# Score products of a first model's attention as two rounded products over stacked key parts

## The chip, the cores and the metric

One core of one Trainium2 chip runs the whole program. The metric is the device time of one execution in microseconds, the median of three executions: 3229.28 us before the change (3226.82, 3229.28 and 3235.23 us). PE is the matmul engine (TensorE), PEld its weight loads, DVE VectorE, ACT ScalarE, POOL GpSimd, SP SyncE. Lines such as L1209 are lines of the kernel before.

## The reference

Two models run one after the other. The first has two layers over 512 main tokens and 256 context tokens. Each layer normalises the tokens, projects them, and mixes them by two convolutions and two attentions; then follow an output projection and a feed-forward part of 16 experts. The change touches the attentions of the first model alone. Each has 4 query heads of 64 channels that share 2 key/value heads. One is global; the other sees keys at most 128 positions away, the context keys, and a learned sink logit:

```python
def gqa_attend(q, k, v, sink=None):
    s = jnp.einsum('bqkgd,bjkd->bkgqj', q, k).astype(jnp.float32) * (HEAD_DIM ** -0.5)
    ...
    p = jax.nn.softmax(s, axis=-1)
    ...
    return jnp.einsum('bkgqj,bjkd->bqkgd', p.astype(v.dtype), v)
def window_attention(q, k, v, kc, vc, sink):
    ...
    valid = (kpos >= 0) & (kpos < s) & (jnp.abs(qpos - kpos) <= WINDOW)
    s_loc = jnp.where(valid[None, :, None, None], s_loc, -jnp.inf)
    sl = jnp.broadcast_to(sink.reshape(N_KV_HEADS, GQ)[None, :, :, None, None].astype(jnp.float32),
                          s_loc.shape[:-1] + (1,))
    p = jax.nn.softmax(jnp.concatenate([s_loc, s_ctx, sl], axis=-1), axis=-1)
```

In the first layer the 256 context tokens are queries too; in the second they are keys alone.

## The kernel before

The program is a list of stages. The five engines walk through it each in its own order, fixed when the program is built, and meet only at semaphores. The change is in the stage `attend`, which occurs twice: layer 0 (281 to 451 us of the profiled execution) and layer 1 (1271 to 1398 us).

`attention_plan` cuts an attend stage into groups. A group is one kind (1 is the global attention, 0 the windowed one with masks and sink), one key/value head `g` with its two query heads, and either the 512 main queries (a main group) or the 256 context queries (a context group). Layer 0 runs eight groups, g0 to g7: the even ones main, the odd ones context, g0 to g3 of kind 1 and g4 to g7 of kind 0. Layer 1 runs four main groups, g0 and g1 of kind 1, g2 and g3 of kind 0. A group's work is:

- Row maxima, `row_scores` on PE and `maximum` on DVE (L2637, L2639). The scores are computed with queries as rows, one unit per query tile and head, and DVE takes the largest of each row. For main groups the operands are rounded copies in fp32r, k_round and q_round (L1171 global, L1175 windowed tiles with the mask product L1177, L1178 context keys); for context groups they are plain f32 (L1163). The units of a group are issued inside the steps of an earlier group: two groups earlier in layer 0, one in layer 1.
- The shift, `turn_shift` on PE (L1189) and `take_shift` on ACT: the negated maxima are turned into a row and copied (L1934) into row 64 of the queries, so that with the row of ones in the keys each score product subtracts the maximum by itself. For kind 0, two exponentials for the sink come first (L1932). PE waits for the copy before the group's first score product.
- Steps, one per tile of 128 keys, two context tiles first and then, in main groups, four main ones. `scores` on PE computes keys by queries in f32 for each head (L1209; L1202 in context groups), in windowed steps plus one mask product per edge, identity by band (L1213); `exponentials` on ACT (L1975) turns them to probabilities; `mix` on PE (L1230) multiplies the values by them, in f32. Scores of step n+1 are issued before the mix of step n. There are four score banks, two per step.
- The outcome: ACT copies the sums (L1953, L1954), DVE divides (L2678, L2680).

Between these, ACT and DVE compute a 31-tap convolution in their spare time: ACT makes products (L1964) that POOL adds up (L3311), DVE does the other half (L2663, L2666), one tap after each maximum and a few after each outcome. `round_operands` on ACT makes the rounded copies of main groups (L1940 keys, L1941 queries): before the first steps for g0 and the next main group, then in step 1 of a main group for a later one.

## Time and profile before

| what | value |
|---|---|
| timed executions | 3226.82, 3229.28, 3235.23 us |
| profiled execution, span from the first to the last instruction | 3215.5 us |
| attend, layer 0 | 281 to 451 us, 170 us |
| attend, layer 1 | 1271 to 1398 us, 127 us |
| PE busy in the whole span | 2983.4 us, 93% |
| DVE, ACT, POOL busy in the whole span | 1100.8, 737.7, 381.7 us |

The profile gives the profiled execution a span and no device time beside it; the median of the timed runs is 13.8 us longer than this span. The two attend stages are 297 us, 9% of the span. An f32 matmul stands in the trace as two records and an fp32r matmul as one; the trace writes f32 in the shape of both. The ends of matmuls are modelled, so a duration of one record is longer than the distance to the next.

### The profile page before, as it was taken

Reading aid. Unit: us, or ns where it says so; the run is one execution under the profiler, and the core shown is the slowest. Engines: PE = TensorE matmul, PEld = TensorE weight load, DVE = VectorE, ACT = ScalarE, POOL = GpSimd, SP = SyncE. Lnnn points to the kernel's source line nnn. Section 1 sums busy time; section 2 is a strip of 40 time slices with the busy share of each in tenths; the row PEclk is TensorE's granted clock in tenths of the full one; section 3 lists DMA queues with packets and bytes.
Section 4 is the critical chain, followed back from the end, with each engine's and each line's share of the span. In section 5 each row is a group of like instructions: output and inputs, shape, how many; then the busy total and the mean of one; then the engine's idle time right before and its main releaser. Section 6 shows DMA issues by size and latency. Waiting matters only on the chain.

```text
span 3215.5 us, 50344 instructions
## 1 busy us (share of the span) xinstructions
PE 2983.4 (93%) x21802; PEld 1880.8 (58%) x21802; DVE 1100.8 (34%) x1930; ACT 737.7 (23%) x1393; POOL 381.7 (12%) x494
## 2 busy tenths in 40 slices
PE   6999989699999998986988888999999999999999
PEld 3645556455555464554433333888865568678887
DVE  4124754211111244643222224322434463232242
ACT  3113651000000133541000002222322362222232
POOL 2022520122222121411000000000000000000000
PEclk8998989799999999997999999999999989999999
DMA  8930033899999810037999996122311202231130
GB/s 342 394 129 1 1 144 120 344 401 409 408 409 408 308 55 1 1 138 290 417 423 423 424 423 252 59 105 79 113 67 55 69 18 79 79 111 65 66 140 30
DMA packets 138400, 626.97 MB, mean 195 GB/s; under 512 B 12592, under 2 KB 19776, under 8 KB 82896
## 3 DMA queue, kind: packets, MB, share of 16 engines
q1 hardware_dynamic: 122064, 577.67, 44.8%
q0 software_dynamic: 16128, 46.18, 4.3%
q8 instruction: 172, 2.82, 0.4%
q14 instruction: 36, 0.29, 0.0%
HBM read 607.36 MB, written 16.45 MB: 194 GB/s over the span
## 4 chain that ended last, share of the span: by engine, by line
PE 42%; DMA 10%; DVE 2%; ACT 1%; issue 1%; SPq 0%; POOL 0%; DVEq 0%; ACTq 0%; POOLq 0%
PE bank L959 19%; DMA slots<-in_w_up_dram 10%; PE bank L1526 7%; PE bank L1714 4%; PE bank L1403 3%; PE bank L1630 3%; PE bank L1283 1%; PE bank L1647 1%; PE bank L1424 1%; PE bank L1658 0%; PE bank L1453 0%; PE bank L1648 0%; SPq L910 0%; PE bank L1060 0%; PE bank L1061 0%
## 5 line engine op out<-in xcount | busy, mean ns | idle before, releaser
L1403 PE MATMUL bank<-slots,HT 128*32 128x256 f32 x8192 | 478.0, 383 | 52.4 <-DMA slots<-in_w_gate_dram 24.2
L1403 PEld LDWEIGHTS bank<-slots,HT 128*32 128x32 f32 x8192 | 265.6, 111 | 269.0 <-issue 62.6
L959 PE MATMUL bank<-hT_high,chunk_high 128*128 128x512 f32 (+2 forms) x736 | 285.1, 387 | 5.3 <-DVE hT_low L2500 5.3
L959 PE MATMUL bank<-hT_high,low_slots 128*128 128x512 f32 (+2 forms) x736 | 287.1, 390 | 0.0
L959 PE MATMUL bank<-hT_low,chunk_high 128*128 128x512 f32 (+2 forms) x736 | 285.5, 388 | 0.0
L2091 ACT ACTIVATE arena<-bank 128x512 f32<-128x512 f32 x32 | 19.1, 597 | 756.2 <-PE bank L1403 433.8
L959 PE MATMUL bank<-slots,HT 128*128 128x512 f32 (+4 forms) x544 | 180.3, 491 | 7.2 <-issue 5.8
L2843 DVE TENSOR_TENSOR arena<-bank,arena 128x512 f32<-128x512 f32 x32 | 22.1, 692 | 441.9 <-ACT arena L2091 441.9
L959 PEld LDWEIGHTS bank<-hT_high,chunk_high 128*128 128x128 f32 x736 | 139.0, 189 | 35.7 <-DVE hT_low L2500 5.7
L959 PEld LDWEIGHTS bank<-hT_low,chunk_high 128*128 128x128 f32 x736 | 138.8, 189 | 32.4 <-issue 0.2
L959 PEld LDWEIGHTS bank<-hT_high,low_slots 128*128 128x128 f32 x736 | 138.7, 188 | 29.7
L2979 DVE TENSOR_TENSOR arena<-bank,arena 128x512 f32<-128x512 f32 x44 | 30.4, 691 | 355.0 <-PE bank L959 355.0
L1424 PE MATMUL bank<-arena,HT 128*32 128x512 f32 x1280 | 148.1, 599 | 3.1 <-DVE HT L2838 3.1
L959 PEld LDWEIGHTS bank<-slots,HT 128*128 128x128 f32 x544 | 96.3, 193 | 84.3 <-issue 69.2
L1526 PE MATMUL bank<-down_high,ffnT_low 128*128 128x512 f32 x352 | 137.6, 391 | 0.0
L1526 PE MATMUL bank<-down_high,ffnT_high 128*128 128x512 f32 x320 | 125.8, 393 | 0.0
L1526 PE MATMUL bank<-low_slots,ffnT_high 128*128 128x512 f32 x320 | 124.2, 388 | 0.0
L1412 PE MATMUL bank<-slots,HT 128*32 128x256 f32 x2048 | 122.4, 379 | 0.0
L2884 DVE TENSOR_TENSOR X<-X,bank 128x1024 f32<-128x1024 f32 x60 | 70.0, 1207 | 149.1 <-PE bank L1453 149.1
L3311 POOL TENSOR_TENSOR HT<-HT,arena 128x512 f32<-128x512 f32 (+1 forms) x90 | 108.1, 1201 | 76.2 <-ACT arena L1964 66.5
L2164 ACT ACTIVATE arena<-bank 128x512 f32<-128x512 f32 x44 | 26.4, 600 | 363.8 <-PE bank L959 363.7
L2961 DVE TENSOR_TENSOR low_slots<-slots,chunk_high 128x1024 fp32r<-128x1024 f32 x88 | 103.4, 1217 | 2.6 <-ACT chunk_high L2142 2.6
(453 smaller groups left out, 4897.4 us busy)
## 6 DMA issues: line engine op xcount, KB each, us to landing
slots<-in_w_gate_dram SPq DMA_DIRECT2D x128, 1024.0 KB, 19.5
slots<-in_w_up_dram SPq DMA_DIRECT2D x128, 1024.0 KB, 21.7
arena<-in_w_down_dram SPq DMA_DIRECT2D x80, 1024.0 KB, 23.3
arena<-in_ada_w_dram SPq DMA_DIRECT2D x48, 1024.0 KB, 9.1
X<-in_w_down_dram SPq DMA_DIRECT2D x32, 1024.0 KB, 18.3
slots<-in_w_in_dram SPq DMA_DIRECT2D x15, 2048.0 KB, 8.9
slots<-in_ffn_w_gate_dram SPq DMA_DIRECT2D x10, 2048.0 KB, 8.5
slots<-in_ffn_w_up_dram SPq DMA_DIRECT2D x10, 2048.0 KB, 8.9
```

The source lines that it names most:

```text
L959: mm = pe.matmul(out_, lhsT, rhs, start=(n == 0), stop=(n == len(pairs) - 1))
L1283: mm = pe.matmul(bank[:, b + j, :], y, part, start=(k == OUT_WHOLE[0]), stop=(k == OUT_LATE[-1]))
L1403: mm = pe.matmul(bank[32 * j:32 * j + 32, 2 + n, 256 * g:256 * g + 256], xT[:, 64 * k + 32 * g:64 * k + 32 * g + 32], columns(w[:, c, :], ...
L1412: mm = pe.matmul(bank[32 * j:32 * j + 32, 4, 256 * n:256 * n + 256], xT_c[:, 32 * k:32 * k + 32], columns(w[:, c, :], j), start=(k == 0 an ...
L1424: mm = pe.matmul(bank[32 * j:32 * j + 32, 5, :], actT[half][:, 2 * q + c, lo:lo + 32], w[:, c, 512 * h:512 * h + 512], start=(q == 0 and c ...
L1526: mm = pe.matmul(bank[:, b, :], x, w_parts[part][:, 512 * half:512 * half + 512], start=(k == 0 and m == 0), stop=(k == F_CHUNKS - 1 and m ...
L1630: mm = pe.matmul(bank[:, j, :], HT[:, k, tile_cols(i)], w[:, k, :], start=(k == 0), stop=(k == KD - 1))
L1647: pe.matmul(bank[:, b, 0:qt * P + P], qT[rows, h, tile_cols(qt)], kT[rows, h, 0:qt * P + P], start=True, stop=False)
L1714: mm = pe.matmul(bank[:, b + n, :], w, x, start=(k == ks[0] and part == 0), stop=(k == ks[-1] and part == 2))
L2884: dve.tensor_tensor(X[:, t, :], X[:, t, :], flat_bank[:, at_spread:at_spread + D], ALU.add).then_inc(sem["spread_taken"], 1)
L2961: dve.tensor_tensor(ffn_columns(low_flat(unit), c), ffn_columns(slot_of(unit), c), chunk_high[:, g % SPLIT_RING, :, :].bitcast(F32), ALU.s ...
L3311: pool.tensor_tensor(dst, other, products[:, n % 4, 0:hi - lo], ALU.add).then_inc(sem["tap_added"], 1)
```

## The change

Each score product, f32 keys by f32 queries, becomes two fp32r products into the same bank. Keys and queries are each split into a rounded part (high) and the rest (low). `k_parts` holds the low part of the keys in partitions 0 to 63 and their high part in 64 to 127; `q_round`, and for context queries the new `c_round`, hold the high part of the queries twice, in both halves. The first product takes all 128 partitions and gives (low + high keys) by high queries. The second takes the high keys with their row of ones by the low queries `q_low`, whose row 64 is now the shift, 65 partitions. Low by low is left out. `k_parts` and `q_low` lie over the f32 keys and queries.

For this, ACT makes two more copies per main group and two for each context group, and DVE subtracts (`low_parts`): two subtractions for a main group, one for a context group. The maxima of context groups use rounded operands too, all maxima leave out row 64, and the mask products use fp32r copies of identity and band, which ACT makes once. `take_shift` copies first, and the sink exponentials read that copy. PE no longer waits for the sink exponentials before the next group's maxima. POOL no longer clears the queries' row 64. The scratch for POOL's DMA descriptors goes from its default to 8192 bytes a partition.

```diff
+        c_round = rounded("c_round", slots_at, first_slots("qkv")[0] % SLOTS * SLOT + 4 * NTOK, 2, 2, CTX)
+        k_parts = rounded("k_parts", arena_at, at_moe, 2, 2, NTOK)
+        q_low = [rounded(f"q_low{l}", slots_at, unit % SLOTS * SLOT, 2, HEADS, NTOK) for l, unit in enumerate(first_slots("w_out"))]
+
+        def q_high(st, group, rows, j):
+
+            if group.main:
+                return q_round[st.layer][rows, group.kind, group.heads + j, :]
+            return c_round[rows, group.turn, j, :]
...
-                    if unit is group.units[0] and group.main:
-                        mains = sum(other.main for other in groups[:group.number + 1])
-                        pe.wait_ge(sem["rounded"], st.at("rounded", 2 * mains))
+                    if unit is group.units[0]:
+                        pe.wait_ge(sem["rounded"], st.at("rounded", group.split_by))
                     if unit is group.units[0] and group.number >= ahead:
                         pe.wait_ge(sem["shift_done"], st.at("shift_done", group.number))
-                        before = 2 * sum(other.kind == 0 for other in groups[:group.number])
-                        if before:
-                            pe.wait_ge(sem["sink_row"], st.at("sink_row", before))
-                    kT = K_ext[0:HD + 1, group.kind, group.g, :]
+                    kT = k_round[st.layer][0:HD, group.kind, group.g, :]
                     if not group.main:
                         for j in range(2):
-                            mm = pe.matmul(bank[:, b, CTX * j:CTX * j + CTX], q_ext[0:HD + 1, group.kind, group.heads + j, tile_cols(qt)],
+                            mm = pe.matmul(bank[:, b, CTX * j:CTX * j + CTX], q_high(st, group, slice(0, HD), j)[:, tile_cols(qt - ST)],
                                            kT[:, SEQ:NTOK], start=True, stop=True)
                         mm.then_inc(sem["rowmax_full"], 1)
...
                     if one.first:
+                        pe.wait_ge(sem["w_split"], st.at("w_split", group.split_by))
                         pe.wait_ge(sem["shift_done"], st.at("shift_done", group.number + 1))
-                    keys = K_ext[0:HD + 1, group.kind, group.g, tile_cols(one.kt)]
+                    both_parts = k_parts[:, group.kind, group.g, tile_cols(one.kt)]
+                    high_part = k_round[st.layer][0:HD + 1, group.kind, group.g, tile_cols(one.kt)]
...
                         if j is None:
-                            pe.matmul(bank[:, b, :].rearrange("p (a n) -> p a n", a=2), keys,
-                                      q_ext[0:HD + 1, group.kind, group.heads:group.heads + 2, SEQ:NTOK],
-                                      start=True, stop=True).then_inc(sem["score_full"], 1)
+                            out_ = bank[:, b, :].rearrange("p (a n) -> p a n", a=2)
+                            pe.matmul(out_, both_parts, c_round[:, group.turn, :, :], start=True, stop=False)
+                            pe.matmul(out_, high_part, low[0:HD + 1, group.kind, group.heads:group.heads + 2, SEQ:NTOK],
+                                      start=False, stop=True).then_inc(sem["score_full"], 1)
                             continue
                         edges = []
                         if group.kind == 0 and one.kt < ST:
                             edges = [(t, 0 if t < one.kt else 1) for t in (one.kt - 1, one.kt + 1) if 0 <= t < ST]
-                        mm = pe.matmul(bank[:, b, 0:one.hi - one.lo], keys, q_ext[0:HD + 1, group.kind, group.heads + j, one.lo:one.hi],
-                                       start=True, stop=not edges)
+                        out_ = bank[:, b, 0:one.hi - one.lo]
+                        pe.matmul(out_, both_parts, q_high(st, group, slice(0, P), j)[:, one.lo:one.hi], start=True, stop=False)
+                        mm = pe.matmul(out_, high_part, low[0:HD + 1, group.kind, group.heads + j, one.lo:one.hi], start=False, stop=not edges)
                         for t, side in edges:
                             lo = P * t - one.lo
-                            mm = pe.matmul(bank[:, b, lo:lo + P], ident[:, :], band[:, side, :], start=False, stop=t == edges[-1][0])
+                            mm = pe.matmul(bank[:, b, lo:lo + P], ident_high[:, :], band_high[:, side, :], start=False, stop=t == edges[-1][0])
                         mm.then_inc(sem["score_full"], 1)
...
                 def take_shift(group):
 
                     n = group.queries[1] - group.queries[0]
+                    shift = q_low[st.layer][HD:HD + 1, group.kind, group.heads:group.heads + 2, group.queries[0]:group.queries[1]]
                     act.wait_ge(sem["shift_full"], st.at("shift_full", group.number + 1))
+                    act.activation(shift, bank[0:1, 4:6, 0:n], ACT.Copy).then_inc(sem["shift_done"], 1)
                     if group.kind == 0:
...
+                        act.wait_ge(sem["shift_done"], st.at("shift_done", group.number + 1))
                         for j in range(2):
-                            act.activation(rows[HD:HD + 1, j, 0:n], bank[0:1, 4 + j, 0:n], ACT.Exp, scale=HD ** -0.5,
-                                           bias=sink[0:1, st.layer, group.heads + j:group.heads + j + 1]).then_inc(sem["sink_row"], 1)
-                    act.activation(q_ext[HD:HD + 1, group.kind, group.heads:group.heads + 2, group.queries[0]:group.queries[1]],
-                                   bank[0:1, 4:6, 0:n], ACT.Copy).then_inc(sem["shift_done"], 1)
+                            act.activation(rows[HD:HD + 1, j, 0:n], shift[:, j, :].bitcast(F32), ACT.Exp, scale=HD ** -0.5,
+                                           bias=sink[HD:HD + 1, st.layer, group.heads + j:group.heads + j + 1]).then_inc(sem["sink_row"], 1)
 
                 def round_operands(group):
 
                     kind, g = group.kind, group.g
-                    act.activation(k_round[st.layer][0:HD + 1, kind, g, :], K_ext[0:HD + 1, kind, g, :], ACT.Copy)                       .then_inc(sem["rounded"], 1)
-                    act.activation(q_round[st.layer][0:HD + 1, kind, 2 * g:2 * g + 2, :], q_ext[0:HD + 1, kind, 2 * g:2 * g + 2, 0:SEQ],
-                                   ACT.Copy).then_inc(sem["rounded"], 1)
+                    q = q_ext[0:HD, kind, 2 * g:2 * g + 2, group.queries[0]:group.queries[1]]
+                    if group.main:
+                        act.activation(k_round[st.layer][0:HD + 1, kind, g, :], K_ext[0:HD + 1, kind, g, :], ACT.Copy)\
+                           .then_inc(sem["rounded"], 1)
+                        q_to = q_round[st.layer][:, kind, 2 * g:2 * g + 2, :]
+                    else:
+                        q_to = c_round[:, group.turn, :, :]
+                    act.activation(q_to[0:HD, :, :], q, ACT.Copy).then_inc(sem["rounded"], 1)
+                    if group.main:
+                        act.wait_ge(sem["rounded"], st.at("rounded", group.split_by - 1))
+                        act.activation(k_parts[HD:P, kind, g, :], K_ext[0:HD, kind, g, :], ACT.Copy).then_inc(sem["w_high"], 1)
+                    act.activation(q_to[HD:P, :, :], q, ACT.Copy).then_inc(sem["w_high"], 1)
...
-                to_round = [group for group in groups if group.main]
-                round_operands(to_round.pop(0))
+                round_operands(groups[0])
+                if ahead == 2:
+                    round_operands(groups[1])
                 take_shift(groups[0])
-                round_operands(to_round.pop(0))
+                round_operands(groups[ahead])
                 if ahead == 2:
                     take_shift(groups[1])
...
-                        if n == 1 and to_round and group.main:
-                            round_operands(to_round.pop(0))
+                        if n == 1 and group.number + ahead + 1 < len(groups):
+                            round_operands(groups[group.number + ahead + 1])
...
+                def low_parts(group):
+
+                    kind, g = group.kind, group.g
+                    cols = slice(*group.queries)
+                    heads = slice(group.heads, group.heads + 2)
+                    if group.main:
+                        dve.wait_ge(sem["w_high"], st.at("w_high", group.split_by - 1))
+                        dve.tensor_tensor(k_parts[0:HD, kind, g, :], K_ext[0:HD, kind, g, :], k_round[l][0:HD, kind, g, :].bitcast(F32),
+                                          ALU.subtract).then_inc(sem["w_split"], 1)
+                        high = q_round[l][0:HD, kind, heads, :]
+                    else:
+                        high = c_round[0:HD, group.turn, :, :]
+                    dve.wait_ge(sem["w_high"], st.at("w_high", group.split_by))
+                    dve.tensor_tensor(q_low[l][0:HD, kind, heads, cols], Q_ext(l)[0:HD, kind, heads, cols], high.bitcast(F32),
+                                      ALU.subtract).then_inc(sem["w_split"], 1)
+
...
                     for unit in group.units:
                         maximum(unit)
+                    if group.number == 0:
+                        low_parts(group)
...
-                    for unit in units:
+                    for n, unit in enumerate(units):
                         maximum(unit)
+                        if n == 1:
+                            low_parts(groups[group.number + 1])
...
-                step(pool.memset(Q_ext(st.layer)[HD:HD + 1, :, :, :], 0.0))
...
-    nc = bacc.Bacc("TRN2", target_bir_lowering=False, num_devices=1)
+    nc = bacc.Bacc("TRN2", target_bir_lowering=False, num_devices=1, dynamic_dma_scratch_size=8192)
```

On ACT in layer 0, around the steps of context group g1 (L1964 or L1991 are taps, L1975 or L2002 exponentials, L1934 or L1944 the shift of g3, L1953 and L1954 or L1980 and L1981 the outcome of g1), before:

```order
L1975 ACTIVATE arena<-bank 128x512
L1934 ACTIVATE slots<-bank 1x2x256
L1964 ACTIVATE arena<-arena,conv_b_w 128x512
L1975 ACTIVATE arena<-bank 128x512 x2
L1953 ACTIVATE arena<-bank 64x256
L1954 ACTIVATE HT<-bank 64x256
L1953 ACTIVATE arena<-bank 64x256
L1954 ACTIVATE HT<-bank 64x256
L1964 ACTIVATE arena<-arena,conv_b_w 128x512 x2
L1975 ACTIVATE arena<-bank 128x512 x2
L1940 ACTIVATE k_round_54<-arena 65x768
L1941 ACTIVATE q_round_56<-slots 65x1024
```

The same place after the change:

```order
L2002 ACTIVATE arena<-bank 128x512
L1944 ACTIVATE q_low_60<-bank 1x2x256
L1960 ACTIVATE k_round_54<-arena 65x768
L1965 ACTIVATE q_round_56<-slots 64x1024
L1968 ACTIVATE k_parts<-arena 64x768
L1969 ACTIVATE q_round_56<-slots 64x1024
L1991 ACTIVATE arena<-arena,conv_b_w 128x512
L2002 ACTIVATE arena<-bank 128x512 x2
```

The copies of main group g4 have moved from step 1 of g2 to step 1 of g1, ahead of the exponentials of g2's first step, and are four instead of two; in step 1 of g2 the two copies of context group g5 take their place.

On DVE in layer 0, at the maxima of context group g3 within g1 (TENSOR_REDUCE is a maximum, SCALAR_TENSOR_TENSOR 128x2 the negation, on HT a tap), after the change; before, the same rows stand there without L2717 and L2723:

```order
L2667 TENSOR_REDUCE small<-bank 128x2
L2694 SCALAR_TENSOR_TENSOR HT<-arena,conv_b_w,HT 128x256
L2667 TENSOR_REDUCE small<-bank 128x2
L2679 SCALAR_TENSOR_TENSOR small<-small 128x2 x2
L2717 TENSOR_TENSOR k_parts<-arena,k_round_54 64x768
L2723 TENSOR_TENSOR q_low_60<-slots,q_round_56 64x2x512
L2694 SCALAR_TENSOR_TENSOR HT<-arena,conv_b_w,HT 128x512
L2706 RECIPROCAL arena<-arena 128x512
```

The low parts of g2 stand behind the second maximum and its negation, ahead of the tap and of the division of g0's outcome.

On PE in layer 0, a windowed step of g4 with one unit of maxima around it, before:

```order
L1209 MATMUL bank<-slots,arena 128x384
L1213 MATMUL bank<-band,ident 128x128 x2
L1209 MATMUL bank<-slots,arena 128x384
L1213 MATMUL bank<-band,ident 128x128 x2
L1175 MATMUL bank<-k_round_54,q_round_56 128x128
```

and after:

```order
L1223 MATMUL bank<-q_round_56,k_parts 128x384
L1224 MATMUL bank<-q_low_60,k_round_54 128x384
L1227 MATMUL bank<-band_high,ident_high 128x128 x2
L1223 MATMUL bank<-q_round_56,k_parts 128x384
L1224 MATMUL bank<-q_low_60,k_round_54 128x384
L1227 MATMUL bank<-band_high,ident_high 128x128 x2
L1185 MATMUL bank<-k_round_54,q_round_56 128x128
```

Nothing has moved past anything else; each f32 score product is two rows.

## Rows read from the trace of the kernel before

**Rows 1.** The page: span, and busy time of each engine.

```profile
span 3215.5 us, 50344 instructions
PE 2983.4 (93%) x21802; PEld 1880.8 (58%) x21802; DVE 1100.8 (34%) x1930; ACT 737.7 (23%) x1393; POOL 381.7 (12%) x494
```

**Rows 2.** Stretches of layer 0's attend: length, PE, PEld, DVE, ACT, POOL busy, PEclk, DMA.

```profile
301.80:323.35 21.55, 21.55 (x59) 10.86 (x58) 13.07 (x20) 7.37 (x12) 0.33 (x1) 0.85 0.00 0
323.35:347.30 23.95, 22.00 (x80) 12.26 (x79) 17.05 (x24) 21.08 (x36) 15.13 (x12) 1.00 0.00 1
347.30:359.30 12.00, 12.00 (x55) 7.16 (x54) 9.52 (x13) 4.33 (x8) 7.89 (x6) 1.00 0.00 0
359.30:381.60 22.30, 17.65 (x59) 9.87 (x59) 19.21 (x24) 19.19 (x34) 14.54 (x10) 0.97 0.00 1
381.60:405.25 23.65, 23.60 (x113) 17.02 (x113) 13.97 (x22) 6.70 (x16) 9.65 (x10) 0.89 0.00 1
405.25:425.60 20.35, 16.73 (x43) 9.75 (x42) 13.34 (x17) 14.87 (x31) 6.44 (x8) 0.75 0.00 0
425.60:440.00 14.40, 14.40 (x62) 9.74 (x61) 0.49 (x1) 8.30 (x20) 8.89 (x13) 1.00 0.01 2
```

**Rows 3.** The same for layer 1's attend.

```profile
1286.70:1310.36 23.66, 23.66 (x62) 11.55 (x61) 13.84 (x19) 7.64 (x13) 0.00 (x0) 0.83 0.00 0
1310.36:1326.30 15.94, 15.94 (x57) 8.54 (x56) 10.37 (x13) 15.37 (x26) 10.90 (x9) 1.00 0.00 1
1326.30:1337.84 11.54, 11.54 (x53) 6.94 (x52) 8.85 (x12) 3.60 (x6) 5.84 (x4) 1.00 0.00 1
1337.84:1352.00 14.16, 12.60 (x46) 6.49 (x45) 13.83 (x11) 13.70 (x24) 9.82 (x7) 1.00 0.00 0
1352.00:1366.84 14.84, 14.79 (x89) 11.43 (x88) 9.21 (x12) 4.11 (x8) 8.31 (x6) 1.00 0.01 1
1379.00:1391.30 12.30, 12.30 (x55) 8.50 (x53) 0.66 (x1) 3.16 (x8) 1.68 (x3) 1.00 0.01 1
```

**Rows 4.** Groups of PE instructions: line, names, shapes, count, busy us, mean ns, idle before.

```profile
L1209 PE MATMUL bank<-slots,arena 65*128 65x512 f32 (+2 forms) x192 | 92.0, 592 | 3.7 <-ACT slots L1934 3.7
...
L1177 PE MATMUL bank<-band,ident 128*128 128x128 f32 x96 | 21.5, 307 | 0.0
...
L1213 PE MATMUL bank<-band,ident 128*128 128x128 f32 x96 | 16.4, 280 | 0.0
...
L1163 PE MATMUL bank<-arena,slots 65*128 65x256 f32 x32 | 11.3, 516 | 3.1 <-DVE small L2637 1.6 <-ACT slots L1934 1.5
```

**Rows 5.** PE in order of time: start, us, line, tile, shape, count.

```profile
395.19 0.61 PE L1213 MATMUL bank<-band,ident 128*128 128x128 f32 x4
...
462.29 0.39 PE L1283 MATMUL bank<-low_slots,out_y_high_a 128*128 128x512 f32 x1
462.52 0.39 PE L1283 MATMUL bank<-out_w_high,out_y_low 128*128 128x512 f32 x1
```

**Rows 6.** PE weight loads of an f32 product, in order of time.

```profile
468.02 0.19 PEld L1283 LDWEIGHTS bank<-slots,HT 128*128 128x128 f32 x1 [0.24 <-issue]
468.45 0.19 PEld L1283 LDWEIGHTS bank<-slots,HT 128*128 128x128 f32 x1 [0.24 <-issue]
```

**Rows 7.** ACT in order of time: the two rounded copies of a main group.

```profile
341.61 0.84 ACT L1940 ACTIVATE k_round<-arena 65x768 fp32r<-65x768 f32 x1
342.35 1.05 ACT L1941 ACTIVATE q_round<-slots 65x1024 fp32r<-65x1024 f32 x1
```

**Rows 8.** Groups of DVE instructions with two tensors from SBUF; the second in layer 0's attend.

```profile
L2592 DVE TENSOR_TENSOR arena<-arena,rope_cos 128x768 f32<-128x768 f32 x8 | 7.7, 958 | 0.3
...
L2680 DVE TENSOR_TENSOR HT<-HT,arena 128x512 f32<-128x512 f32 x4 | 4.0, 996 | 0.1
```

**Rows 9.** One microsecond at a time, PE alone: length, PE busy, PEclk.

```profile
378.00:379.00 1.00, 0.00 (x0) 1.00 0.00 0
...
380.00:381.00 1.00, 1.00 (x6) 0.57 0.00 0
```

20 lines of the change are left out of this document (15 added, 5 removed).

## The prediction

> **What bounds the kernel now.** I read the page first, then the two attend stages in stretches cut where the limiting engine changes, then the PE groups in them, then the distances between instructions. The span is 3215.5 us, and PE is busy in 93% of it [rows 1]. The stretches say more. In four of layer 0's seven, and in the stretches of layer 1 from 1286.70, 1310.36, 1326.30, 1352.00 and 1379.00, PE has hardly an idle moment [rows 2, 3]. But three other stretches have another limit. From 323.35 ACT is busy 21.08 of 23.95 us. From 359.30 ACT and DVE are busy 19.19 and 19.21 of 22.30 us, and PE only 17.65. From 1337.84 DVE and ACT are busy 13.83 and 13.70 of 14.16 us. From 1310.36 ACT has 15.37 of 15.94 us, so there PE and ACT are level. The change takes work from PE and gives work to ACT and DVE: it pays in the first sort of stretch and costs in the second.
>
> **What PE saves.** An f32 product is two records; loads of one in dense work stand 468.45 - 468.02 = 0.43 us apart for 512 columns [rows 6], so a product costs 0.86 us at full clock. An fp32r product of 512 columns is one record, and two of them start 462.52 - 462.29 = 0.23 us apart [rows 5]. Two of these in place of one f32 product save 0.40 us. By columns, 384 save 0.30 and 256 save 0.20. A maximum product of 256 columns goes from 0.43 to 0.12: 0.31. For a mask product, four f32 records take 0.61 us, and 0.28 of it is the length of the last [rows 4, 5]: 0.11 a record, 0.22 a product, and one fp32r record of 0.11 to 0.14 saves about 0.09.
> Counts: L1209 has 192 records, 96 products; by the plan these are 64 of 512 columns, 16 of 384 and 16 of 256. Context groups have 8 more of 512, L1163 has 16 products and the masks 96 (192 records) [rows 4]. So 72 x 0.40 + 16 x 0.30 + 16 x 0.20 + 16 x 0.31 + 96 x 0.09 = 50 us. About ten score products and half of L1163's run at half clock, where each saves as much again: 57 us in all. This is the most that can be had.
>
> **What ACT and DVE get.** A main group's copies cost 0.84 and 1.05 us, started 0.74 us apart [rows 7], so four take about 3.75 instead of 1.9. Two copies of a context group, half as wide as the queries' copy, take about 1.2. With eight main and four context groups that is 8 x 1.9 + 4 x 1.2 = 20 us more on ACT. On DVE a subtraction of 768 columns takes 0.96 us [rows 8] and one of 1024 columns, in proportion, 1.28: 2.2 us for each of eight main groups, about 0.65 for each of four context groups, 20 us in all. No row shows a subtraction of this shape on 64 partitions. A lower bound is the 2.2 us; for the upper one the L2680 row is nearest: with POOL at work its mean was 0.996 us for 512 columns, which makes 3.5 us. I take 2.2 and keep 3.5 for the range.
> The GPSIMD Engine Reference of the Trainium skill (section Specifications) says that POOL shares its SBUF interfaces with VectorE and contends with instructions that read two tensors from SBUF. The trace agrees with the L2680 row; were every subtraction to meet POOL, this would be the upper bound, some 5 us more in the sum.
>
> **Layer 0, by stretches** [rows 2].
> (a) To 323.35: PE bound. Context maxima at the front run at half clock: 8 products, 4 of them ahead of the first shift, save 2.5 us. Of g0's score products 12 stand here, six at half clock: 6 x 0.4 + 6 x 0.8 = 7.2. Against it, ACT has two more copies ahead of the first exponentials, 1.9 us. -8.
> (b) From 323.35: ACT bound. g4's copies come in whole (3.75), and g5's 1.2 stand where 1.9 stood; the wait for g3's shift behind PE shrinks by two products, 0.8. +2.3.
> (c) From 347.30: PE bound. Six score products (2.4) and some sixteen masks (1.4). -4.
> (d) From 359.30: ACT and DVE bound. g6's four copies (3.75) and g7's two (1.2) come in, 4.95 us; ACT was idle for 22.30 - 19.19 = 3.1 us of the stretch, and I let two of them take it up: +2.9. DVE's 2.2 us for g4 run beside that.
> (e) From 381.60: PE bound with DVE busy 13.97 of 23.65 and ACT 6.70, so the cover holds. Four products of 384, four of 256, two of 512, some 22 masks, part of it at half clock: -5.
> (f) From 405.25: a chain from ACT's outcome of g4 over one mix to the next shift; half a score pair at half clock: -1.
> (g) From 425.60: PE bound. Four of 384, four of 256, one of 512, fourteen masks: -3.5.
> Sum -16.3. The tail behind, ACT and DVE's last outcome, does not change.
>
> **Layer 1** [rows 3].
> (a) To 1310.36: by PE alone -5, but DVE binds before that. Its 13.84 us of maxima and taps begin only with the first mix, which stands several us into the stretch, and become 16.0 with the subtractions; the shift of g1 waits for the last maximum. What is left is the earlier start, as the first mix no longer stands behind f32 scores at half clock: -2.2.
> (b, c) 1310.36 to 1337.84: ACT gets 1.9 us more in (b), PE needs 1.2 us less in each beat of (c), DVE has 27.48 - 19.22 = 8.3 us idle, mostly at the front, and takes 2.2. -3.
> (d) From 1337.84: ACT and DVE bound, nothing added to either. 0.
> (e) From 1352.00: DVE 9.21 of 14.84, so 5.6 us idle, less 2.2: -3.4, PE's own saving here being 4.2.
> (f) 1366.84 to 1379.00: ACT bound: 0. (g) From 1379.00: -2.5 by products of 384 and 256 and the masks.
> Sum -11.1. Both layers: -27.4.
>
> **The clock.** PE idled all of 378 to 379 us, and from 380 the granted clock was at half, 1.2 of 2.4 GHz [rows 9]; the stretch from 381.60 has a mean of 0.89 [rows 2], so 2 x 0.11 x 23.65 = 5.2 us at half and 2.6 us lost. With PE faster and ACT not, PE will idle more in (b) and (d) of layer 0 and from 1310.36. I allow one more such fall, +2.4. Total -25: a span of 3190.5, and with the 13.8 us between the span and the median of 3229.28 us a time of 3204 us.
> The page TensorE: Matmul & The Clock Gate (section HAM oscillation) of the Trainium skill states the rule against this change: idle gaps throw the PE clock back to half, and work in bursts then runs cold again and again. Rows 9 agree on one gap; how many the change makes, no row shows.
>
> **No cost.** The copies of identity and band are two short ones on ACT in the projection stage, where it waits for PE. Dropping POOL's clearing frees an engine that was waiting. The smaller descriptor scratch has no row; POOL's DMAs are gathers and loads well apart, and I put nothing on it. If it held POOL up, the gathers of the experts would be late and the time after 451 us would grow.
>
> **Rivals.**
> (R1) The whole of PE's saving comes through, ACT and DVE hiding all: -57, 3172 us. For it: PE is hardly idle in four of seven stretches of layer 0 and in most of layer 1. Against: the full ACT and DVE in (b) and (d).
> (R2) ACT and DVE in series eat nearly all: their 20 us each fall on the path in turn wherever a group's shift waits for both, and PE's saving in PE-bound stretches is cut to what DVE leaves. Of layer 0's -22 in (a), (c), (e), (g) half stays, -11, with +5 and +5 in (b) and (d), and layer 1 comes to -5: -6 with subtractions at 3.5, 3223 us. For it: DVE's taps follow each maximum, whatever PE does.
> (R3) The clock, slower than before: PE, waiting for ACT in each group's front, stays at half clock into the PE-bound stretches. About 215 us of PE work are left in the two stages; each microsecond of it at half clock costs one more. From 27 us beyond what is cold now the gain is gone; if 50 us are, the time is 3229 - 27 + 50 = 3252 us. For it: rows 9. Against: the stretch from 323.35 has idle PE and a clock of 1.00.
> (R4) A product over rounded parts costs as much as an f32 record, 0.43: the scores then save nothing, and only masks and context maxima do, 14 us, against 7 us more of ACT where it binds, and 3 us of masks that it hides: 3225 us. The 0.23 of rows 5 speaks against it.
>
> **Chances and range.** Forecast 0.60, R1 0.08, R2 0.19, R3 0.08, R4 0.05. The forecast's own range is 3192 to 3217 (PE-bound stretches two thirds as good or a third better, subtractions at either bound, none or three more falls of the clock). The range of 8 in 10 reaches toward R1 and past R2: 3181 to 3226. 0.3% is 9.7 us, about what a measurement of this kernel tells from no change: faster than 3219.6 is nearly all of the forecast, R1, and a third of R2: 0.73. Within 0.3%: most of R2, a little of the forecast and of R4: 0.16. Slower: R3 and the rest: 0.11.
>
> **What would show it.** Distances of 0.23 us between the two products of a pair (against R4); L1209's 92 us of records replaced by some 192 records of fp32r; ACT busy nearly throughout the stretches that follow the shifts of g2 and g4 and these longer by 2 to 3 us; PE with gaps there, and half clock in one place more than before; DVE without idle time between maxima in g0 of layer 1; attend about 154 us in layer 0 and 117 in layer 1, plus the clock; everything outside the two stages as long as before. The prediction is wrong if the stages shrink by less than 10 or more than 40 us together, or if time changes after 451 us outside attend.

## The result and the profile after

The changed kernel took 3263.95 us, median of 4 runs (3247.02 to 3272.16); the kernel before took 3229.44 us beside it. The ratio is 1.0098, with a 95% interval of 1.0073 to 1.0123: slower by 1.0%, where the prediction said 3204 us. The profiled execution took 3272.16 us, 1.9 us more than its span. The page of the changed kernel, whose counterpart is [rows 1]:

```profile
span 3270.3 us, 50164 instructions
PE 3013.4 (92%) x21690; PEld 1892.7 (58%) x21690; DVE 1125.8 (34%) x1950; ACT 757.0 (23%) x1419; POOL 378.5 (12%) x492
```

PE has 112 records fewer and is busy 30 us longer than in [rows 1]. Of these, 13 us lie in the attends and 15 between them, and those 15 belong to the execution that [rows 1] shows, as the next lines tell. The changed kernel by stages (from the start of layer 0's attend to the end of layer 1's); columns as in [rows 2], and the row in the middle is what lies between the two attends:

```profile
277.60:460.30 182.70, 149.29 (x456) 86.98 (x456) 113.39 (x144) 106.86 (x193) 93.72 (x87) 0.79 0.01 3
460.30:1300.00 839.70, 784.68 (x8716) 438.76 (x8716) 221.40 (x453) 115.25 (x241) 139.07 (x204) 0.96 0.73 287
1300.00:1441.80 141.80, 127.24 (x368) 71.79 (x368) 82.38 (x86) 74.70 (x123) 59.54 (x44) 0.76 0.01 1
```

The same three stretches of a second profile of the kernel before (run e5_before_again), and the middle one of the first profile:

```profile
276.20:445.60 169.40, 150.33 (x520) 89.64 (x520) 100.46 (x133) 95.19 (x178) 88.71 (x87) 0.87 0.01 3
445.60:1284.20 838.60, 783.59 (x8716) 443.64 (x8716) 221.46 (x453) 115.19 (x240) 144.08 (x205) 0.96 0.74 288
1284.20:1407.70 123.50, 113.19 (x416) 65.86 (x416) 70.23 (x78) 67.78 (x115) 57.80 (x44) 0.90 0.01 1
```

```profile
448.50:1270.10 821.60, 769.74 (x8716) 431.43 (x8716) 221.44 (x453) 115.26 (x241) 144.08 (x205) 0.96 0.74 294
```

The attends grew by 13.3 and 18.3 us, together 31.6; the medians differ by 34.5. The middle is level, 839.7 against 838.6. The profile that the prediction read was a rare execution, some 18 us short in the middle, so its span lay 13.8 us under the median, and this belonged to that execution, not to what lies around a span.

Where the attends grew, by stretches that end at the same transposes (L1199, L1189 before): the one from 316.20 answers to [rows 2] from 323.35 to 359.30 (35.95 us), the one from 1341.90 to [rows 3] from 1310.36 to 1337.84 (27.48 us).

```profile
316.20:364.60 48.40, 40.58 (x117) 21.68 (x117) 28.31 (x39) 28.36 (x47) 23.43 (x17) 0.82 0.00 0
...
1341.90:1378.80 36.90, 36.28 (x97) 18.59 (x97) 21.92 (x26) 20.76 (x33) 16.38 (x12) 0.77 0.00 0
```

In the second one PE is idle for 0.62 us only, and yet it takes 9.4 us more. A granted clock of 0.77 means that 17 of its 36.9 us ran at half clock and lost 8.5. What is left, 27.8 us, is what the stretch took before at full clock (27.48). So PE's own work did not shrink as predicted, and a large part ran at half clock.

**One account for all runs.** The runs of the next section appear here already. I cut both attends at each change of the granted clock and read PE's busy time in every piece. The length is then a sum of three: PE's work at full clock (busy at full, plus half of busy at half), what the half clock cost (the other half), and PE's idle time. Work here is busy time, stalls inside it included. Both attends together, us, from one profile each; times are medians. "maxima" is the row count of the maximum products, "split" tells which engines did the split's work (unused: done, but PE does not read it; left out: not done), "cold" is what the half clock cost.

```
run                   maxima  split       time    length  work   cold  idle
before, 2nd profile   65      -           3230    292.9   233.5  30.1  29.4
changed               64      ACT, DVE    3264    324.5   211.7  64.9  47.9
e6  max64             64      -           3261    325.8   265.7  33.5  26.6
e8  masks, ctx        65      -           3224.5  286.6   218.2  38.6  29.9
e9  masks, ctx, 64    64      -           3274    343.4   245.1  69.8  28.6
e3  f32 scores        64      unused      3307    367.9   244.9  78.7  44.3
e4  no split          64      left out    3250    306.8   211.4  57.0  38.4
e7  65, no split      65      left out    3201    262.0   187.1  32.4  42.4
e12 ACT copies        65      ACT only    3209    270.6   187.4  34.3  49.0
e14 unwaited          65      unused      3234    285.8   187.5  41.9  56.5
e1  65 rows           65      ACT, DVE    3233    295.1   188.6  43.4  63.1
e10 65, f32 masks     65      ACT, DVE    3233    300.8   198.8  41.1  61.0
e11 keys later        65      ACT, DVE    3226    286.2   190.1  34.6  61.4
e13 POOL              65      ACT, POOL   3208    277.2   188.1  31.5  57.6
```

From before to the changed kernel: work -22 instead of the -50 of the prediction, half clock +35 instead of +2.4, idle +18.5. The sum is +31.6. One profile is one execution: outside the attends, where these kernels hardly differ, the sixteen profiled executions took between 2923 and 2947 us. Medians of times and lengths of single profiles can therefore differ by some 10 us.

### The profile page after: what moved, and what is told of

Its sections match the earlier page's. It is cut to its first block, busy times and chain, and to the rows that moved or that the text cites. A ratio compares the mean times of both kernels' runs of the same rounds, so it can differ in the third digit from the quotient of the medians.

```text
span 3270.3 us, 50164 instructions
## 1 busy us (share of the span) xinstructions
PE 3013.4 (92%) x21690; PEld 1892.7 (58%) x21690; DVE 1125.8 (34%) x1950; ACT 757.0 (23%) x1419; POOL 378.5 (12%) x492
## 4 chain that ended last, share of the span: by engine, by line
PE 42%; DMA 10%; DVE 2%; ACT 1%; issue 1%; SPq 0%; POOL 0%; DVEq 0%; ACTq 0%; POOLq 0%
PE bank L974 19%; DMA slots<-in_w_up_dram 9%; PE bank L1540 7%; PE bank L1728 4%; PE bank L1417 3%; PE bank L1644 2%; PE bank L1297 1%; PE bank L1661 1%; PE bank L1438 1%; DMA slots<-in_w_gate_dram 1%; PE bank L1672 1%; PE bank L1662 0%; PE bank L1467 0%; PE bank L1075 0%; PE bank L1076 0%
## 5 line engine op out<-in xcount | busy, mean ns | idle before, releaser
L1417 PE MATMUL bank<-slots,HT 128*32 128x256 f32 x8192 | 492.4, 385 | 54.9 <-DMA slots<-in_w_gate_dram 28.9
L1244 PE MATMUL bank<-arena 128*128 128x512 f32 (+2 forms) x224 | 121.5, 672 | 23.4 <-ACT HT L1981 15.6
L1426 PE MATMUL bank<-slots,HT 128*32 128x256 f32 x2048 | 130.0, 379 | 0.7
```

The costliest lines, as they stand in the source:

```text
L1244: mm = pe.matmul(bank[:, 6 + j, lo:hi], V_ext[:, one.kt, group.kind, at_v:at_v + P], p, start=one.first, stop=ends)
L1417: mm = pe.matmul(bank[32 * j:32 * j + 32, 2 + n, 256 * g:256 * g + 256], xT[:, 64 * k + 32 * g:64 * k + 32 * g + 32], columns(w[:, c, :], ...
L1426: mm = pe.matmul(bank[32 * j:32 * j + 32, 4, 256 * n:256 * n + 256], xT_c[:, 32 * k:32 * k + 32], columns(w[:, c, :], j), start=(k == 0 an ...
```

## Experiments

**Rows of the maxima.** The diff has one edit that the prediction gave no term: the maximum products multiply 64 rows (`0:HD`) where they multiplied 65. PE in one beat of the changed kernel at full clock, where windowed maxima are made: four score products and one unit of maxima with its masks; columns start, us, line, tiles, shape, count:

```profile
349.82 0.50 PE L1223 MATMUL bank<-q_round,k_parts 128*128 128x512 f32 x1
350.16 0.40 PE L1224 MATMUL bank<-q_low,k_round 65*128 65x512 f32 x1
350.40 0.40 PE L1223 MATMUL bank<-q_round,k_parts 128*128 128x512 f32 x1
350.64 0.40 PE L1224 MATMUL bank<-q_low,k_round 65*128 65x512 f32 x1
350.97 0.33 PE L1185 MATMUL bank<-k_round,q_round 64*128 64x128 f32 x1
351.23 0.33 PE L1187 MATMUL bank<-band_high,ident_high 128*128 128x128 f32 x1
351.48 0.44 PE L1185 MATMUL bank<-k_round,q_round 64*128 64x128 f32 x2
351.85 0.33 PE L1187 MATMUL bank<-band_high,ident_high 128*128 128x128 f32 x1
352.11 0.39 PE L1188 MATMUL bank<-k_round,q_round 64*128 64x256 f32 x1
352.42 1.98 PE L1244 MATMUL bank<-arena 128*128 128x512 f32 x4
```

and in the kernel before:

```profile
346.72 1.88 PE L1209 MATMUL bank<-slots,arena 65*128 65x512 f32 x4
348.03 0.62 PE L1175 MATMUL bank<-k_round,q_round 65*128 65x128 f32 x1
...
349.13 0.36 PE L1178 MATMUL bank<-k_round,q_round 65*128 65x256 f32 x1
349.33 1.88 PE L1230 MATMUL bank<-arena 128*128 128x512 f32 x4
```

Both beats are 2.6 us long (352.42 - 349.82 and 349.33 - 346.72): nothing is saved. Within a run of 128 and 65 rows the products do start 0.24 us apart, near the 0.23 of the prediction. But each step from 65 or 128 rows to 64, or back, costs some 0.1 us: 0.34 at the first score product, 0.33 at the first maximum, 0.25 from a maximum to its mask and again from the mask to the next. The page TensorEngine Tiling (Array Packing) of the Trainium skill says in its section Key Properties that a change of tiling mode drains TensorE, and lists 64 rows as a mode of its own in the section Available Configurations. The rows agree with it, and the prediction should have weighed it.

Run e1_rows65, with the order of two ACT copies changed since its maxima wait for one of them:

```
- kT = k_round[...][0:HD, ...]       q = q_high(st, group, slice(0, HD), ...)
+ kT = k_round[...][0:HD + 1, ...]   q = q_high(st, group, slice(0, HD + 1), ...)
```

> The changed kernel, but the maximum products multiply 65 rows instead of 64 (the 65th row of the queries' operand is the copy of query row 0, so each maximum and with it the shift is off by that query value, which the softmax cancels); the upper copy of the queries stands ahead of that of the keys on ACT, so that the maxima can wait for it. T1 (products of 64 rows beside products of 65 or 128 rows cost about 0.1 us at every change, and each mask among maxima has two such changes): in a local group four score products and one row's maxima, 2.60 us now, take about 1.9 us; PE's work at full clock in the two attends falls from 212 us to about 185; the time falls by 5 to 25 us from 3264, since ACT and DVE then bound more. T2 (fp32r products of this size cost that in themselves, row count regardless): spacings 0.33 and 0.25 us stay, time within 8 us of the changed kernel's 3264.

Measured: 3233.18 us, 1.0009 of before (0.9997 to 1.0022), work 188.6. The beat, its maxima first:

```profile
348.52 0.62 PE L1185 MATMUL bank<-k_round,q_round 65*128 65x128 f32 x1
348.99 0.28 PE L1187 MATMUL bank<-band_high,ident_high 128*128 128x128 f32 x1
349.10 0.39 PE L1185 MATMUL bank<-k_round,q_round 65*128 65x128 f32 x2
349.32 0.27 PE L1187 MATMUL bank<-band_high,ident_high 128*128 128x128 f32 x1
349.43 0.33 PE L1188 MATMUL bank<-k_round,q_round 65*128 65x256 f32 x1
349.60 0.40 PE L1223 MATMUL bank<-q_round,k_parts 128*128 128x512 f32 x1
349.84 0.40 PE L1224 MATMUL bank<-q_low,k_round 65*128 65x512 f32 x1
350.08 0.39 PE L1223 MATMUL bank<-q_round,k_parts 128*128 128x512 f32 x1
350.31 0.39 PE L1224 MATMUL bank<-q_low,k_round 65*128 65x512 f32 x1
350.68 0.33 PE L1185 MATMUL bank<-k_round,q_round 65*128 65x128 f32 x1
```

A mask now stands 0.11 us ahead of the next product instead of 0.25, and the first and the last of the four score products start 0.71 us apart instead of 0.82. The beat takes 2.2 us (350.68 - 348.52) instead of 2.6, where T1 expected 1.9; PE's work is near T1's 185. T1 holds and T2 falls, but the time fell by more than the 5 to 25 us of T1: 31 us of the 34 are gone by the row count.

Run e6_max64 puts the edit alone into the kernel before:

```
- kT = k_round[st.layer][0:HD + 1, ...]    q = q_round[st.layer][0:HD + 1, ...]
+ kT = k_round[st.layer][0:HD, ...]        q = q_round[st.layer][0:HD, ...]
```

> The kernel before with one edit: the maximum products multiply 64 rows instead of 65 (the 65th adds zero). T1 (a change between 64 rows and 65 or 128 costs about 0.1 us on PE; f32 products around it): PE's work at full clock in the attends grows from 234 us by 10 to 25, and the time from 3232 by 10 to 30. If the row count costs only beside fp32r products of 128 rows: no change within 4 us.

Measured: 3261.19 us, 1.0092 (1.0072 to 1.0112); work +32, above what T1 expected, and time +31, at its upper end. One row fewer in the main groups' maxima makes the kernel before as slow as the changed one.

**The clock.** Run e9_masks_ctx_64 has 64-row maxima, rounded masks, f32 scores and none of the split's work; run e8_masks_ctx is the same with 65 rows. Both, against before:

```
- pe.matmul(scores_of_tile, ident[:, :], band[:, ...], ...)
+ pe.matmul(scores_of_tile, ident_high[:, :], band_high[:, ...], ...)
...
- kT = K_ext[0:HD + 1, ...]; q_ext[0:HD + 1, ...]        (context maxima)
+ kT = k_round[...][0:rows, ...]; c_round[0:rows, ...]   (rows: 64 in e9, 65 in e8)
```

> Masks and context maxima from rounded operands with 64-row maxima, f32 scores, nothing added to ACT and DVE but the context groups' copy. With 65 rows this took 3224.5, with 64-row maxima and f32 masks 3261; the changed kernel's waits with f32 scores took 3307 and had 181 us at half clock in the attends. If the waits for ACT and DVE make the half clock: 3250 to 3262, half clock in the attends under 90 us. If PE falls to half clock by itself where 64-row products and fp32r masks alternate in small pieces: 3280 or more, half clock above 130 us.

> Masks and context maxima from rounded operands alone, over 65 rows; scores stay one f32 product, no subtractions and no upper copies. The terms of the sum for these two: 16 x 0.31 + 96 x 0.09 = 14 us of PE against 2.4 us more on ACT; in the path's stretches that would be 5 to 9 us: 3224 to 3228. If a mask as an fp32r product costs what the f32 one did (0.22 us, bound by its weight load) and the context maxima stand where PE waits: 3230 to 3235.

Measured: e9 3273.75 us (3253.11 to 3283.75), 1.0117; e8 3224.51 us, 0.9985 (0.9971 to 0.9999). The time at half clock in the two attends, of which the column "cold" is about a half, was 68 us before (second profile), 75 in e6, 85 in e8 and 150 in e9. Two stretches of e9 and one of the changed kernel:

```profile
339.50:351.10 11.60, 11.60 (x34) 5.52 (x33) 5.58 (x8) 8.24 (x15) 9.19 (x7) 1.00 0.00 0
351.10:368.20 17.10, 17.10 (x28) 7.68 (x28) 4.83 (x6) 3.62 (x6) 4.49 (x4) 0.50 0.00 0
```

```profile
348.52 0.33 PE L1186 MATMUL bank<-band_high,ident_high 128*128 128x128 f32 x1
348.77 0.38 PE L1187 MATMUL bank<-k_round,q_round 64*128 64x256 f32 x1
349.08 1.98 PE L1220 MATMUL bank<-slots,arena 65*128 65x512 f32 x4
```

```profile
402.50:419.60 17.10, 17.10 (x42) 11.26 (x43) 7.94 (x13) 3.33 (x8) 3.94 (x5) 0.50 0.00 0
```

PE idled nowhere in the 11.6 us before the fall of e9 nor in the 17.1 us after it. What it did there was maxima and masks with row changes, 1.4 us in each beat (from 347.64 to 349.08 in the last one), between f32 products of 1.9 us. So the clock fell without an idle gap, where PE's busy time held many 64-row changes and small fp32r products; the profile counts the stalls as busy. Each of the two alone does little: e6 has the row changes with f32 masks (cold 33.5), e8 the fp32r masks with 65 rows (38.6), both together 69.8. (In e6 the context groups' maxima stay f32 products of 65 rows; in e9 they are rounded and have 64.)

The times say the same: +31 in e6, -6 in e8, and +43 instead of +25 in e9. Over all runs the size is less sure than in these profiles: what the half clock cost in a whole execution, worked out from span and granted clock, was by the medians 4 us more than before in e6, 9 in e8 and 28 in e9, with 127 to 167 us in the four single runs of e9. e9's time lies between its two expectations; its half clock is on the side of PE itself. For e8 the first case came true.

The page TensorE: Matmul & The Clock Gate of the Trainium skill (section HAM oscillation), which the prediction cited on the clock, explains such falls by idle gaps. The changed kernel has such gaps, this one on the way to its stretch above:

```profile
388.09 3.75 PE L1244 MATMUL bank<-arena 128*128 128x512 f32 x4 [3.41 <-ACT HT L1981]
```

The clock fell within that gap. But it came back, and its fall at 402.5 stands behind 14.4 us in which PE was busy without a break. So gaps account for some falls, but not for this one and that of e9.

Run e3_f32_scores: the changed kernel, with

```
- pe.matmul(out_, both_parts, q_high(...), start=True, stop=False)
- mm = pe.matmul(out_, high_part, low[0:HD + 1, ...], start=False, ...)
+ mm = pe.matmul(out_, K_ext[0:HD + 1, ...], q_ext[0:HD + 1, ...], start=True, ...)
```

> The changed kernel with its score products as single f32 products of 65 rows, as before, and every wait, copy and subtraction of the change kept (their results are written beside the operands and not used; copies and subtractions work on 32 partitions where the operands are in place). If PE's saving on the scores is real and large (the prediction: 0.40 us per product): slower than the changed kernel by 20 us or more, about 3290. If the new score products save little (0 to 0.2 us a product) and the clock falls because PE is left waiting: PE stays busy longer between waits, the half clock in the attends falls from 151 us toward the 74 of before, and the time is equal to the changed kernel's or below, 3245 to 3265.

Measured: 3307.39 us, 1.0233. The score products' saving is real: work 244.9 against 211.7, 33 us. The clock did not recover with a busier PE (cold 78.7), so the second case of the expectation falls.

Run e10_65_f32_masks, e1 with `ident`, `band` in place of `ident_high`, `band_high`:

> The run with 65 rows (3233) with the masks as f32 products again. PE's work at full clock grows by 96 x 0.1 = 10 us by the distances (0.11 against 0.20 to 0.22 us a mask). If small fp32r products let the clock fall: half clock in the attends falls from 113 us to under 90, and the time stays within 4 us of 3233 or falls. If the clock follows the waits: half clock within 15 us of 113, time 3236 to 3243.

Measured: 3233.08 us, 1.0007 (0.9997 to 1.0016), as e1. Work +10.2, that is 0.11 a mask. The time at half clock was 103 us against 113, which is the second case's, and the time is the first one's; with 65 rows the masks' form decides nothing. (No diff is shown: it is these two names, at both places.)

**The split's work.** Run e4_no_split (both products from the rounded parts, no upper copies, no subtractions) and the same with 65 rows, e7_65_no_split:

```
- pe.matmul(out_, both_parts, q_high(st, group, slice(0, P), j)[...], start=True, stop=False)
+ pe.matmul(out_, high_part, q_high(st, group, slice(0, HD + 1), j)[...], start=True, stop=False)
...
- act.activation(k_parts[HD:P, ...], ...); act.activation(q_to[HD:P, ...], ...)
- low_parts(group)
```

> The changed kernel's PE program with two fp32r products per score (both over 65 rows of the rounded parts, so the scores are twice the rounded product), but without the upper copies on ACT and without the subtractions on DVE and the waits for them: the split is left out. If the added work of ACT and DVE and the waits for it make the gaps and with them the half clock: the attends shrink to about 160 and 120 us and the time falls to 3210 to 3225. If a PE that is faster than ACT falls to half clock by itself: half clock stays over 110 us in the two attends and the time stays above 3240.

> As the run without the split (two fp32r products per score over 65 rows of the rounded parts, no upper copies, no subtractions), but with 65 rows in the maxima too: PE's whole saving with nothing added to ACT and DVE except the context groups' copy. The split, and so the scores' low part, is left out. If ACT's and DVE's added work is what turns the remaining saving into idle time and half clock in the run with 65 rows (3233): 3200 to 3215, idle PE in the attends under 50 us. If PE's own speed does it (it then waits for ACT's exponentials): 3222 to 3232, with half clock above 80 us in the attends as before.

Measured: e4 3250.40 us, 1.0068; e7 3201.06 us, 0.9901 (0.9881 to 0.9920). e4 gave its second case (126 us at half clock), but the reason named there, a PE faster than ACT, falls with e7, where PE is faster still and is at half clock for 75 us: the row count kept the rest. With e1 and the changed kernel these make a square: 64 rows cost 31 us with the split and 49 without; the split costs 14 with 64 rows and 32 with 65. That the split's work costs less with 64 rows fits a PE that is held up by itself and so hides added work of others. e7's work is 187.1, 46 less than before: PE's saving was well sized, less the row count.

Run e12_act_copies is e7 with ACT's upper copies put back, run e14_subtract_unwaited is e12 with DVE's subtractions too, unused and not waited for:

```
+ act.activation(k_parts[P - 32:P, ...], K_ext[0:32, ...], ACT.Copy)    (e12, e14)
+ act.activation(q_to[P - 32:P, ...], q[0:32], ACT.Copy)
...
+ dve.tensor_tensor(k_parts[P - 32:P, ...], ..., ALU.subtract)          (e14)
+ dve.tensor_tensor(q_low[l][P - 32:P, ...], ..., ALU.subtract)
```

> The run with 65 rows and without the split (3201), with ACT's upper copies put back (32 rows each, same columns; their results are not used), still without the subtractions and without any wait for them. The split's work costs 32 us in all (3233 against 3201). If ACT carries it: 3218 to 3230. If DVE's subtractions and the waits for them carry it: 3202 to 3210.

> The run with ACT's upper copies and no split (3209), with DVE's subtractions put back at their places (32 rows, same columns; results unused), PE not waiting for them. Together with PE's wait they cost 24 us (3233 against 3209). If DVE's time in front of maxima and outcomes does it: 3225 to 3233. If PE's wait for the low parts does it: 3209 to 3215.

Measured: e12 3209.43 us, 0.9936; e14 3234.34 us, 1.0006. By the medians ACT's copies cost 8 us and DVE's subtractions 25, and the same with PE's wait for their result is e1's 3233, so the wait adds nothing. The lengths of the attends, one profile each, divide it otherwise: 9 for the copies (262.0 to 270.6), 15 for the subtractions (285.8) and 9 for the wait (295.1). The two steps together cost 24 us either way; how they share it stays open. DVE's groups in the changed kernel; columns line, names, shapes, count, busy, mean ns:

```profile
L2723 DVE TENSOR_TENSOR q_low<-slots,q_round 64x1024 fp32r<-64x1024 f32 x8 | 15.5, 1944 | 0.0
L2717 DVE TENSOR_TENSOR k_parts<-arena,k_round 64x768 fp32r<-64x768 f32 x8 | 9.0, 1129 | 0.0
L2723 DVE TENSOR_TENSOR q_low<-slots,c_round 64x512 fp32r<-64x512 f32 x4 | 3.6, 905 | 0.0
```

28 us in all where I had 20: 3.07 us a main group, between my 2.2 and the bound of 3.5. The mean mixes two cases, here in layer 1:

```profile
1311.35 2.28 DVE L2723 TENSOR_TENSOR q_low<-slots,q_round 64x1024 fp32r<-64x1024 f32 x1
...
1325.61 1.21 DVE L2723 TENSOR_TENSOR q_low<-slots,q_round 64x1024 fp32r<-64x1024 f32 x1
```

POOL was at work beside the first one nearly throughout and had no instruction beside the second. Of the eight, the two without POOL took 1.21 us each and the six with it 1.74 to 2.29. This fits the contention with POOL that the prediction kept for its range, though no run takes POOL's work away. In e14 they have the same columns on 32 partitions and took 33 us (DVE is busy 207 us in the two attends, 173 in e12), so its cost may be somewhat too high.

**Order and engine.** Run e11_keys_later is e1 with the keys' upper copy one step later; run e13_pool_split is e11 with the later groups' subtractions between POOL's tap sums.

```
- round_operands(groups[group.number + ahead + 1])                    (n == 1)
+ round_operands(groups[...], later=len(group.steps) > 2)             (e11, n == 1)
+ upper_keys(groups[group.number + ahead + 1])                        (e11, n == 2)
...
- dve.tensor_tensor(k_parts[0:HD, ...], ..., ALU.subtract)            (e13, groups from ahead on)
+ pool.tensor_tensor(k_parts[0:HD, ...], ..., ALU.subtract)
```

> The run with 65 rows (3233), with the upper copy of the keys one step later than the other three copies of its group, so that ACT does not hold a step's exponentials and the outcome behind four copies in a row. If the waits of PE for ACT (18 us idle ahead of the mixes in layer 0) come from the copies' bunching: 3222 to 3230. If it is ACT's and DVE's total that binds: 3231 to 3235.

> The run with 65 rows and the keys' copy later (3226), with the subtractions of all groups but those ahead (two in layer 0, one in layer 1) taken from DVE and put between POOL's tap sums, at the point of its program that ACT's taps have reached when the copies are made. If DVE's time is what binds: 3205 to 3218. If the subtractions' result is then late, since POOL is slower (about 4.5 us for a main group by its 1.26 us per 512 columns) and stands behind taps: 3230 or more, with PE waiting for q_low longer than the 10 us in the run with 65 rows.

Measured: e11 3226.36 us, 0.9993 (0.9980 to 1.0006), its first case, though no sure gain over before or over e1 (0.9997 to 1.0022), and not at the place that it named: layer 1's attend went from 133.3 to 123.3 us, layer 0's stayed; e13 3208.18 us, 0.9926 (0.9909 to 0.9943), its first case and faster than both kernels. POOL needs more time for the same subtraction, and it had that time:

```profile
L3390 POOL TENSOR_TENSOR q_low<-slots,q_round 64x1024 fp32r<-64x1024 f32 x6 | 15.5, 2577 | 0.0
...
L3385 POOL TENSOR_TENSOR k_parts<-arena,k_round 64x768 fp32r<-64x768 f32 x6 | 11.7, 1952 | 18.5 <-ACT k_parts L1974 18.4
```

**Outside the attends.** Run e2_scratch is the kernel before with `dynamic_dma_scratch_size=8192`, run e5_before_again the kernel before itself.

> The kernel before with the 8192-byte descriptor scratch as its only edit. If the scratch holds POOL's DMAs up: the stages between the attends take about 837 us instead of 819 and the time grows by 10 to 20 us from 3229. If what was seen outside the attends (22 us between two single profiles) is spread between executions: same time within 5 us, and the stages between the attends anywhere in 815 to 840 us.

> The kernel before once more, for a second profile of it. If the 18 us that the first profile is shorter between the attends are a rare execution: the stages between them take 836 to 842 us here as in the four other profiles, the attends again 169 and 123 us, and the span is 3225 to 3236. If they are the kernel's own: about 822 us.

Measured: e2 3232.74 us, 1.0002 (0.9993 to 1.0012), 840.4 us between its attends; e5 3225.29 us, 838.6 us between them. The scratch costs nothing, as predicted, and the 18 us were the first execution's.

## Why the prediction was wrong

- **What PE saves.** This is the step that failed. It counted products and columns, and passed over the row count of the maxima. The score products' spacing of 0.23 us held (R4 falls), and so did 50 us as a size: 45 were there with 65 rows (e1), 15 of them by masks and context maxima, where I had 14 (e8). With 64 rows 23 of these are lost, and "-4" for [rows 2] from 347.30 and "-3.4" for [rows 3] from 1352.00 had no ground, since a beat with windowed maxima stays at 2.6 us. In place of -50 the changed kernel has -22, and the row count alone costs 31 us of time (e1, e6).
- **The clock.** I allowed 2.4 us; it was 35, and 21 of these go with the row count (64.9 in the changed kernel, 43.4 in e1). R3 came out by its sign and near its price (3252 against 3264), but only in a small part by its mechanism: I had PE idling for ACT and staying cold afterwards. One fall stands in such a gap (3.41 us, before 388.09). But the longest cold piece behind those with which both attends begin (as they did before), 17.1 us from 402.50, has PE busy throughout and before it, and e9 has the falls with nothing added to ACT or DVE but the context groups' copies.
- **What ACT and DVE get.** ACT's 20 us were right: two more copies of 0.84 and 1.04 us a main group. DVE's were mis-sized, 28 for 20; the long subtractions are those with POOL at work. The larger error is where they fall: I let them cost 5 us in (b) and (d) and hid them elsewhere; with PE at its new speed they cost 32 us (e1 against e7), nearest to R2 (3223 against 3233) for the kernel with 65 rows. R2 had no term for the clock, though, and 13 us of e1's are that. Its -22 for (a), (c), (e) and (g) should read -20.5, which moves it by less than 1 us.
- **Stretches.** The time from 323.35 to 359.30 [rows 2] was to change by -1.7 us (+2.3 - 4) and grew by 12.4. PE's first stretch, to 323.35, was to shrink by 8 and shrank by 5.5 (277.60 to 316.20 now). It has the maxima over all keys, 512 columns wide, and so few row changes.
- **No cost.** The scratch was free (e2). The copies of the masks and the dropped clearing stood in no run by themselves, and nothing outside the attends shows a cost of them (the first one starts at 277.6 us, against 276.2 in e5; 839.7 us lie between them, against 838.6). The 13.8 us between span and median were this execution's; they moved the start of the sum, not the difference.
- **The forecast's size.** A kernel with PE's saving and none of the split's work, e7, took 29 us less than before, where I gave 25 to the whole change. R1's cover, ACT and DVE hiding everything, was not there even then: idle time grew by 13 us.

What stays open: by which measure of activity the clock falls in a busy PE, how the subtractions and PE's wait for them share 24 us, and the rest between e13 (3208) and e7 (3201).

## What to carry to other kernels

Read the row counts of neighbouring matmuls in a diff, not only their types and columns: one row fewer, 64 for 65, cost this kernel 30 us by itself. A busy PE is no proof of work; compare the distance between starts of the same beat, and the granted clock, in both kernels. And when an engine gets faster, price the work added to the others at the new speed; here moving DVE's part to POOL, slower by a third to three quarters but idle, won 18 us (e11 to e13).

## Not expected of the hardware

- A change between 64 and 65 or 128 rows on PE costs some 0.1 us at full clock (0.25 us instead of 0.11 from a mask to the next product), and the profile counts it as busy.
- The granted clock fell to half with PE busy all of the 11.6 us before and stayed there for 17.1 us of full busy time, where 64-row fp32r products and fp32r masks of 128 columns alternate between f32 products; with the row changes alone the time at half clock grew by 7 us, with the fp32r masks alone by 17, with both by 82 (one profile each).
- A subtraction of two tensors from SBUF on DVE took 1.21 us for 1024 columns on 64 partitions without POOL beside it and up to 2.29 with POOL at work, 1.94 in the mean, and 1.95 in the mean on 32 partitions (e14); on POOL it took 2.58.
- Of sixteen profiled executions, with no change there but the scratch, one had 821.6 us between the attends and the others 835 to 840.
